# Order of banks, turned rows and splits around two norms of a two-block transformer kernel

## The reference, cut to what matters

```python
kv_shift, kv_scale = split(c_act @ kv_ada_w + kv_ada_b)             # between the layers
sh1, sc1, g1, sh2, sc2, g2 = split(c_act @ ada_w[l] + ada_b[l], 6)   # for each layer
# layer 0, behind the convolution
x = layer_norm(ALPHA * x + (1 + g1) * out, ln_g[0, 0], ln_b[0, 0])   # "ln0"
h = x * (1 + sc2) + sh2                                              # "ffnin"
f = (silu(h @ w1) * (h @ w3)) @ w2                                   # w1, w3: 1024 x 2816
x = layer_norm(ALPHA * x + (1 + g2) * f, ln_g[0, 1], ln_b[0, 1])     # "ln1"
# layer 1
h_kv = x * (1 + kv_scale) + kv_shift;  k, v = split(h_kv @ w_kv)     # "kv"
h = x * (1 + sc1) + sh1;               q = h @ w_q                   # "q"
```

## Time and profile before

| what | value |
|---|---|
| time of the runs | 2295.94, 2297.45, 2300.1 us; median 2297.45 |
| span of the profiled execution | 2299.4 us, 1.95 above the median; no other time is given for that execution |
| busy: PE, PEld, DVE, ACT, POOL | 2211.6, 1898.5, 1722.4, 1379.6, 89.0 us |
| granted TensorE clock, mean | 0.983 |
| loads | 614.26 MB read, 268 GB/s over the span |

### The profile page before, as it was taken

One profiled execution on the slowest core, in us unless ns is written; L12 is line 12 of the kernel. 1 busy time (PEld: TensorE's weight loads), 2 busy tenths in 40 slices (PEclk: granted clock), 3 DMA queues, 4 the chain that ended last, 5 costly groups with the idle time before them and its releaser, 6 DMA issues.

```text
span 2299.4 us, 36465 instructions
## 1 busy us (share of the span) xinstructions
PE 2211.6 (96%) x14714; PEld 1898.5 (83%) x14714; DVE 1722.4 (75%) x1682; ACT 1379.6 (60%) x1296; POOL 89.0 (4%) x164
## 2 busy tenths in 40 slices
PE   7998999998999999999999999999998898999998
PEld 5777999887788888888888888888997797888887
DVE  3875444646788888888988888885777367899966
ACT  3244433545677777777777777774465334777754
POOL 7400000001000000000000000000000000000000
PEclk9999999999899999999999999999999899999999
DMA  9785754666499999999999999996841141899960
GB/s 334 240 267 192 239 183 165 203 213 194 169 351 392 370 373 370 370 371 372 371 369 369 374 367 375 369 371 105 203 137 38 35 170 70 324 372 375 366 217 19
DMA packets 339968, 618.80 MB, mean 269 GB/s; under 512 B 24813, under 2 KB 165944, under 8 KB 339800
## 3 DMA queue, kind: packets, MB, share of 16 engines
q1 hardware_dynamic: 338992, 616.13, 76.6%
q10 hardware_dynamic: 808, 0.30, 0.1%
HBM read 614.26 MB, written 1.05 MB: 268 GB/s over the span
## 4 chain that ended last, share of the span: by engine, by line
PE 75%; DVE 3%; ACT 2%; issue 1%; DVEq 0%; ACTq 0%
PE bank L1281 11%; PE bank L1282 11%; PE bank L1283 11%; PE bank L1314 6%; PE bank L1315 6%; PE bank L1313 6%; PE bank L2196 3%; PE bank L2197 3%; PE bank L2198 3%; PE bank L1254 1%; PE bank L1291 1%; PE bank L600 1%; PE bank L1348 1%; PE bank L2310 1%; PE bank L2301 1%
## 5 line engine op out<-in xcount | busy, mean ns | idle before, releaser
L1400 DVE TENSOR_TENSOR ring_lo<-ring_raw,ring_hi 128x2048 fp32r<-128x2048 f32 x432 | 988.1, 2291 | 138.7 <-ACT ring_hi L1393 138.3
L1393 ACT ACTIVATE ring_hi<-ring_raw 128x2048 fp32r<-128x2048 f32 x432 | 828.0, 1920 | 296.9 <-PE bank L1283 180.7
L1281 PE MATMUL bank<-ring_hi,xg_hi 128*128 128x512 f32 x1152 | 457.7, 397 | 2.7 <-DVE xg_lo L1600 2.1
L1283 PE MATMUL bank<-ring_lo,xg_hi 128*128 128x512 f32 x1152 | 450.6, 391 | 0.0
L1282 PE MATMUL bank<-ring_hi,xg_lo 128*128 128x512 f32 x1152 | 450.6, 391 | 0.0
L476 DVE TENSOR_TENSOR ring_lo<-ring_raw,ring_hi 128x2048 fp32r<-128x2048 f32 (+1 forms) x96 | 218.1, 2281 | 124.0 <-ACT ring_hi L458 116.1
L2196 PE MATMUL bank<-Hh,ring_hi 128*128 128x256 f32 x936 | 268.1, 286 | 7.2 <-DVE ring_lo L476 5.9
L2198 PE MATMUL bank<-Hh,ring_lo 128*128 128x256 f32 x936 | 266.3, 284 | 0.0
L2197 PE MATMUL bank<-Hl,ring_hi 128*128 128x256 f32 x904 | 257.3, 285 | 0.0
L1281 PEld LDWEIGHTS bank<-ring_hi,xg_hi 128*128 128x128 f32 x1152 | 217.2, 189 | 48.4 <-ACT xg_hi L1457 2.8
L1283 PEld LDWEIGHTS bank<-ring_lo,xg_hi 128*128 128x128 f32 x1152 | 216.9, 188 | 47.1
(11 more groups left out here) (514 smaller groups left out, 2872.5 us busy)
## 6 DMA issues: line engine op xcount, KB each, us to landing
ring_raw<-in_moe_w SPq DMA_DIRECT2D x672, 512.0 KB, 5.2
ring_raw<-in_ada_w SPq DMA_DIRECT2D x96, 512.0 KB, 5.2
ring_raw<-in_ffn_w SPq DMA_DIRECT2D x66, 512.0 KB, 4.9
ring_raw<-in_exp_gate SPq DMA_DIRECT2D x64, 512.0 KB, 4.7
ring_raw<-in_exp_up SPq DMA_DIRECT2D x64, 512.0 KB, 4.7
ring_raw<-in_exp_down SPq DMA_DIRECT2D x64, 512.0 KB, 4.8
ring_raw<-in_w_in SPq DMA_DIRECT2D x42, 512.0 KB, 5.1
ring_raw<-in_conv_in_w SPq DMA_DIRECT2D x16, 512.0 KB, 8.7
```

Of the source, the lines that this page charges most:

```text
L1281: mm(o, xg_hi[:, g, kk, :], wh(k), start=(kk == 0), stop=False)
L1283: last = mm(o, xg_hi[:, g, kk, :], wl(k), start=False, stop=(kk == KT - 1))
L1393: nc.scalar.activation(ring_hi[:, at % SPLIT, :], ring_raw[:, n % RAW, :], ACT.Copy)\
L1400: nc.vector.tensor_tensor(ring_lo[:, at % SPLIT, :], ring_raw[:, n % RAW, :], ring_hi[:, at % SPLIT, :].bitcast(F32), ALU.subtract).then_i ...
```

## The change

1. TensorE takes the four accumulator banks at the first way down (`ffn_down(0)`) and no longer ahead of `ffn a 0`.
2. The last two key-value rows are turned behind `ffn a 0` and no longer ahead of it. ScalarE copies them behind the fourth and the sixth block of `affine_hi` and no longer ahead of the first. The last argument of `row_out` also keeps these two from looking two units ahead for splits.
3. VectorE splits `ffn b 0` in the hole of the norm, behind `ffn a 0`, and no longer behind the norm.
4. Behind the second norm VectorE splits `k 2` behind the fold, splits `k 3` between the third and the fourth pair of the queries' maps, and splits `v 0` ahead of `xT`.
5. ScalarE splits `k 3` and `v 0` behind `Gh`, ahead of its loop over the keys.

```diff
@@ -2409,11 +2409,9 @@
             ln_stats("ln0", tA, summed=True)
             for j in range(4, 8):
                 adaptive(2, j, None)
-            for _ in range(2):
-                turn_row(lambda l, p: b3[:, 4 * p:4 * p + 4])
 
             pe.stage = "ffn"
-            acc = [take(pe, f"ffn acc {i}", "D") for i in range(4)]
+            acc = []
             late = list(range(4))
 
             def turned(l, p):
@@ -2423,6 +2421,8 @@
 
             def ffn_down(j):
                 n = at_unit[("ffn2", j)]
+                if j == 0:
+                    acc.extend(take(pe, f"ffn acc {i}", "D") for i in range(4))
                 pe.eng.wait_ge(*T.at(f"fh {j}"))
                 pe.eng.wait_ge(*T.at(f"fl {j}"))
                 ready(n)
@@ -2451,6 +2451,8 @@
                     columns(("ffn a", j), f"ffn a {j}", Hh, Hl)
                 else:
                     columns_by_block([(("ffn a", 0), "ffn a 0")], Hh, Hl, "ffnin")
+                    for _ in range(2):
+                        turn_row(lambda l, p: b3[:, 4 * p:4 * p + 4])
                 columns(("ffn b", j), f"ffn b {j}", Hh, Hl)
                 if j:
                     ffn_down(j - 1)
@@ -2598,9 +2600,9 @@
                 run(stat[:, 0, :], ps("lv " + name)[:, 0:S], ACT.Sqrt, bias=eps[:, 0:1]).then_inc(act.tick(f"ev lv {name}"), 1)
                 T.mark(f"std {name}", *act.last)
 
-            def affine_hi(name, of, dst):
-
-                for k in range(KT):
+            def affine_hi(name, of, dst, blocks=range(KT)):
+
+                for k in blocks:
                     act.eng.wait_ge(*T.at(f"normed {of} {k // 2}"))
                     g, b = affine_of(name, k)
                     run(dst[:, k, :], tA[:, k, :], ACT.Identity, scale=g, bias=b).then_inc(act.tick(f"hi {name} {k}"), 1)
@@ -2728,9 +2730,11 @@
             gated(0, 2, "conv_out", "out0", True)
             split_hi(act, at_unit[("ffn b", 0)])
             ln("ln0")
-            for p in (2, 3):
-                row_out(2, p)
-            affine_hi("ffnin", "ln0", Hh)
+            affine_hi("ffnin", "ln0", Hh, range(0, 4))
+            row_out(2, 2, 0)
+            affine_hi("ffnin", "ln0", Hh, range(4, 6))
+            row_out(2, 3, 0)
+            affine_hi("ffnin", "ln0", Hh, range(6, KT))
             act.stage = "ffn"
             late = list(range(4))
             for j in range(NP + 1):
@@ -2771,6 +2775,7 @@
             act.eng.wait_ge(*T.at("fold q"))
             affine_hi("q", "ln1", Gh)
             T.mark("Gh q", *act.last)
+            split_hi(act, at_unit[("v", 0)])
             for j in range(4):
                 split_hi(act, at_unit[("k", j)] + 2)
                 act.eng.wait_ge(*T.at(f"mm k {j}"))
@@ -2947,9 +2952,9 @@
                 dve.eng.wait_ge(*dve.own())
                 tt(dst[:, s, :], f[:, s, :], hi[:, s, :].bitcast(F32), ALU.subtract).then_inc(dve.tick(f"lo {name} {j}"), 1)
 
-            def affine_lo(name, f, dst, hi):
-
-                for j in range(4):
+            def affine_lo(name, f, dst, hi, pairs=range(4)):
+
+                for j in pairs:
                     map_pair(name, f, j)
                     low_pair(name, f, dst, hi, j)
 
@@ -3116,9 +3121,8 @@
             tt(gb[:, :], cols[:, :, ROW["conv_out_b"]], mods[:, VEC(0, 2), :], ALU.mult).then_inc(dve.tick("gb"), 1)
             fold_in("ffnin")
             residual("ln0", "out0", "conv_out")
-            ln("ln0", None, lambda: split_lo(dve, at_unit[("ffn a", 0)]), ("ffnin", tD, Hl, Hh))
+            ln("ln0", None, lambda: split_lo(dve, at_unit[("ffn b", 0)]), ("ffnin", tD, Hl, Hh))
             T.mark("Hl ffn", *dve.last)
-            split_lo(dve, at_unit[("ffn b", 0)])
             biased("turn kv", [(2, 0), (2, 1)])
             affine("ln_g", "ln_b", 0)
             dve.stage = "ffn"
@@ -3145,14 +3149,16 @@
             ln("ln1", low=("kv", tD, Hl, Hh))
             dve.stage = "attn"
             T.mark("Hl kv", *dve.last)
-            split_lo(dve, at_unit[("k", 2)])
             biased("turn 1 1", [(1, 1)])
             dve.eng.wait_ge(*dve.own())
             fold_in("q")
             dve.eng.wait_ge(*dve.own())
-            affine_lo("q", tB, Gl, Gh)
+            split_lo(dve, at_unit[("k", 2)])
+            affine_lo("q", tB, Gl, Gh, range(0, 3))
+            split_lo(dve, at_unit[("k", 3)])
+            affine_lo("q", tB, Gl, Gh, range(3, 4))
             T.mark("Gl q", *dve.last)
-            split_lo(dve, at_unit[("k", 3)])
+            split_lo(dve, at_unit[("v", 0)])
             affine("ln_g", "ln_b", 1)
             for key in ("k", "v", "q"):
                 for j in range(4):
```

## The result

The changed kernel takes 2285.17 us (median of 4 runs, 2283.94 to 2291.2) against 2297.97 (4 runs, 2295.94 to 2300.1): 12.8 us less, a ratio of 0.9942 with an interval of 0.993 to 0.9953. On another chip, five runs gave 0.9943 (0.9929 to 0.9957). The prediction was 2285 within 2281 to 2291, faster.

A forecast was written before the change was run, and what follows sets the result against it. TensorE bounds the kernel, its work being 75% of the span, so only its stalls and slow clock offer gains. Terms of -7.0 and -5.65 make -12.7 us, taking 2297.45 to 2284.8, said as 2285, range 2281 to 2291.

The forecast's parts named there:

- The first stall: Ahead of `ffn a 0`: TensorE waits 9.0 us for `mods` of L3057 because a bank is taken too early.
- Term one: From the first norm to `ffn b 0`, which starts at 205.3 instead of 212.34 us: -7.0 us.
- the rows' 1.75 us: Turning the key-value rows behind `ffn a 0` puts some 1.75 us on TensorE's path, formerly run under the norm.
- The slack of 0.3 us at `ffn a 1`: VectorE's low half ends at 210.8, TensorE wants it at 211.1 us; +0.5 us kept as the bound.
- Term two: Second stall, between `k 2` and `k 3`: 4.10 us of wait and 1.55 of slow clock go, -5.65 us.
- The slack reckoned as 1.2 us: At `k 3`: VectorE's low half ends at 435.1 us, TensorE wants it at 436.33.
- Rival 1: The clock is lost in the bursts of `ffn a 0`; term one shrinks by about 3, to 2288 us; chance 0.10.
- Its -9.8 us for that case: The sum instead of -12.7 us if short bursts between waits at `ffn a 0` each run cold.
- Rival 2: One of the two stalls comes back: 2291.8 us with term two alone, 2290.4 with term one alone; chance 0.09.
- Rival 3: In the first experts, DMA loads that don't move set the time and the gain is lost: 2297 us; chance 0.06.
- Rival 4: Slower: the clock falls before `ffn a 0` and stays low over the first units; four give 2303.5 us; chance 0.03.
- The signs: Right: among others, `v 0` some 12.7 us earlier than 447.74. Wrong: among others, a new TensorE wait in a later stage.

The follow-up runs named there:

- banks alone: Against the kernel before, only the take of the accumulator banks moved to the first way down: 2292.81 us, ratio 0.9966.
- first edits: Parts 1 to 3 of the change alone, around the first norm, against the kernel before: 2292.01 us, ratio 0.9961.
- filler: The kernel before with 17 idle matmuls added between `k 2` and `k 3`: 2298.61 us, ratio 0.9991.
- `xT` twice: The changed kernel with the eight `xT` operations of the feed-forward's norm made twice: 2292.98 us, ratio 0.9966 to the kernel before.
- ScalarE's split only: The kernel before with only ScalarE's split of `k 3` and `v 0` moved ahead of its loop over the keys: 2295.87 us, ratio 0.9982.

## Why the prediction was right, step by step

- *The first stall is the bank's.* Shown by the banks alone: -7.32 us, where all of the first edits give -7.21.
- *Term one, -7.0.* -7.21. The added split in the pause was to cost 0.1 and cost nothing: the reciprocal starts 3.22 us later, exactly as all else. Its rows also let the raw slot of `ffn b 0` come free 204.86 - 191.3 = 13.6 us earlier, not 11; nothing hangs on that. The distance taken from `ple`, 12.2 from the reciprocal to the end of `ffn a 0`, came out as 206.64 - 194.44 = 12.2, the turning as 1.71.
- *Where the prediction counted right but judged too little.* It wrote the rows' 1.75 us on the path as part of the price and left it there. The experiments show that this edit is a loss of 0.95 us and that the split in the pause gives nothing beside it, while it gives 0.84 us beside rows that are turned early. Parts 2 and 3 of the change together cost 0.1 us; the gain of term one is the bank's.
- *The slack of 0.3 us at `ffn a 1`.* It was some 0.15 and just held (`ffn a 1` starts 5.83 behind `ffn b 0`, where 5.76 is the least). "Each us that VectorE is later costs up to one" was too mild: with the clock it was 4.20 for 2.63.
- *Term two, -5.65.* -5.64. The slack reckoned as 1.2 us was 432.42 - 430.80 = 1.6. But 1.5 of the term is the clock's, which the filler measured at 1.50 by itself; one execution with the stall kept its full clock, and from its 31.91 us to 28.12 the gain is 3.8 us. The prediction took the one profile for all.
- *The closeness of the number.* The prediction said 2285 and the median is 2285.17, but the four runs lie from 2283.94 to 2291.2 and the interval of the ratio is some 2.6 us to either side. Both terms are borne out by distances; that the total agrees to 0.2 us is luck, as no run resolves it so finely.
- *Rival 1, the clock lost in the bursts.* It was not: the granted clock is 1.00 over 196 to 206 us, with a wait of 1.81 us ahead of the first burst and of 0.44 and 0.51 ahead of the next two. The Trainium skill, "TensorE: Matmul & The Clock Gate", section on HAM oscillation in real kernels, has short bursts run cold when each wait between them is longer than the burst. The waits between the bursts here are shorter than a burst (about 1.4 us), so these rows don't contradict it; the prediction held them against a case that isn't theirs. Its -9.8 us for that case is worked out nowhere; by its own rival 1 (206.6 - 203.5 = 3.1 us less) it is -9.6. Behind the first stall's wait of 8.97 us (8.96 once), TensorE came back to the full clock after a differing time: to `b 0` it is 21.12, 21.23, 21.55 and 21.98 us in four kernels whose code is the same up to there. Against 13.91 that makes term one 7.2 to 8.1 us, and the prediction's profile had the least of them. The Trainium skill, the same page, Part 1 on the clock gate, says that the number of matmuls that run cold varies from run to run; these four agree.
- *Rival 2, a stall that comes back.* No; both distances hold in all kernels that have the edits.
- *Rival 3, given back later.* "Rest" is 1851.2 against 1851.7, and lies between 1849.0 and 1851.9 in all kernels but one (1846.4), with no order by which stall went. The gain stays, as was said; that it does because the ring couples the loads to TensorE wasn't tested by itself.
- *Rival 4.* Its mechanism exists, as `xT` twice shows (2.48 us of wait, then half the clock), but for one unit and 1.57 us, not four.
- *The signs.* `v 0` stands 9.56 us ahead of 447.74, and 12.78 when the 3.22 us from the convolution's norm are taken off. "A TensorE wait in a later stage that wasn't there" exists: behind 1900 us the experts' matmuls wait 1.8 us for `ring_lo` (L1281). But that wait is also in the profiles of the banks only, of ScalarE's split only and of the filler, and not in that of the first edits only, so it doesn't follow the change, and "rest" doesn't show it.

## What to carry to other kernels

A wait stands where the instruction list puts it, not where its operand is used: look at the engine's longest wait, find which resource in program order asked for it, and move only that request; here moving one request gave all that the four edits around the first norm gave. Work moved out of an engine's pause onto its path can be a loss even where it removes a wait (0.95 us here), so try each part by itself; the narrow work did best between bursts that wait for their operands anyway. Where the slack of the next unit is a few tenths of a microsecond, lateness can cost more than itself, because the clock may fall (4.20 us for 2.63 here).

## What the runs showed of the hardware that was not expected

At the second stall a pause of 3.58 us was followed by the full clock in one execution (1.00), and pauses of 3.92 and 3.93 us by half of it, 1.2 GHz, in two others. Elsewhere less was enough for a fall: 2.48 us ahead of `ffn a 1` with `xT` made twice, and 2.49 us in the convolution's norm of the changed kernel; 1.84 us at that same place was not (banks only). So the length of a pause alone, in one profile, doesn't tell whether another execution or another place pays for it. Between executions of the same code this made the distance to `b 0` differ by up to 0.86 us and the one to `v 0` by 1.48 of the 1.85, and in the convolution's norm it cost the profiled execution of the changed kernel 1.51 of its 3.22 us.
